# Triangular inverses of an RWKV-7 layer: half of each stream's blocks cross to the other column half

## The reference, cut to what matters

```python
def step(S, inp):
    r_t, w_t, k_t, v_t, a_t, b_t = inp
    sa = jnp.einsum('bhij,bhj->bhi', S, a_t)
    S = S * w_t[:, :, None, :] + sa[..., None] * b_t[:, :, None, :] + v_t[..., None] * k_t[:, :, None, :]
    return S, jnp.einsum('bhij,bhj->bhi', S, r_t)
```

## Time and profile before

| | us |
|---|---|
| median of 3 runs | 769.61 |
| the runs | 768.45, 769.61, 1230.0 |
| profiled execution | 766.94 |
| its span | 764.9 |
| first pair of inverses | from about 122.5 to 150.1 |
| second pair | from about 149.2 to 176.7 |

### The profile page before, as it was taken

One profiled execution on the slowest core, in us unless ns is written; L12 is line 12 of the kernel. 1 busy time (PEld: TensorE's weight loads), 2 busy tenths in 40 slices (PEclk: granted clock), 3 DMA queues, 4 the chain that ended last, 5 costly groups with the idle time before them and its releaser, 6 DMA issues.

```text
span 764.9 us, 18829 instructions
## 1 busy us (share of the span) xinstructions
PE 739.7 (97%) x7940; PEld 694.8 (91%) x7940; DVE 510.9 (67%) x780; ACT 378.5 (49%) x584; POOL 70.4 (9%) x50
## 2 busy tenths in 40 slices
PE   7999999998999999999999999998999999999997
PEld 6988888987879999999999999875689999999997
DVE  4896985677453788785555677776657887854441
ACT  6656454211443545554444435759966554543331
POOL 0000005090130000000000010015410000000000
PEclk9999999999999999999999999999999999999999
DMA  9954330000111589867666563500055666576651
GB/s 298 275 172 135 97 100 27 5 3 2 58 57 56 164 213 254 236 198 219 194 192 194 168 189 111 166 1 2 2 161 169 198 188 198 186 221 194 194 163 56
DMA packets 111038, 109.25 MB, mean 143 GB/s; under 512 B 7264, under 2 KB 109920, under 8 KB 110848
## 3 DMA queue, kind: packets, MB, share of 16 engines
q1 hardware_dynamic: 110976, 108.35, 47.3%
HBM read 107.29 MB, written 1.05 MB: 142 GB/s over the span
## 4 chain that ended last, share of the span: by engine, by line
PE 87%; DVE 6%; ACT 5%; issue 1%; DMA 1%; POOL 1%; ACTq 0%; SPq 0%; POOLq 0%; DVEq 0%
PE ps L460 66%; PE ps L676 4%; ACT SB L1469 2%; DVE Gs L1722 1%; PE ps L773 1%; ACT PT L1480 1%; PE ps L575 1%; PE ps L762 1%; PE ps L988 1%; PE ps L1007 1%; DVE LT L1748 1%; PE ps L558 1%; DMA xtok<-in_x 1%; POOL t L2141 1%; PE ps L491 1%
## 5 line engine op out<-in xcount | busy, mean ns | idle before, releaser
L1537 DVE TENSOR_TENSOR wlo<-raw,whi 128x1024 fp32r<-128x1024 f32 x188 | 225.9, 1224 | 87.9 <-ACT whi L1130 85.6
L1130 ACT ACTIVATE whi<-raw 128x1024 fp32r<-128x1024 f32 x124 | 130.3, 1058 | 127.3 <-PE ps L460 122.4
L460 PE MATMUL ps<-xh,whi 128*128 128x256 f32 x896 | 178.1, 280 | 1.9 <-DVE xl L2100 1.0
L460 PE MATMUL ps<-xl,whi 128*128 128x256 f32 x896 | 175.4, 277 | 0.0
L460 PE MATMUL ps<-xh,wlo 128*128 128x256 f32 x896 | 175.2, 277 | 0.0
L460 PEld LDWEIGHTS ps<-xh,whi 128*128 128x128 f32 x896 | 135.4, 188 | 6.0 <-issue 4.8
L460 PEld LDWEIGHTS ps<-xl,whi 128*128 128x128 f32 x896 | 135.5, 188 | 0.0
L460 PEld LDWEIGHTS ps<-xh,wlo 128*128 128x128 f32 x896 | 135.3, 188 | 0.0
L1365 ACT ACTIVATE whi<-raw 128x1024 fp32r<-128x1024 f32 x64 | 68.0, 1063 | 78.1 <-PE ps L460 57.3
L460 PE MATMUL ps<-hl,whi 128*128 128x256 f32 x512 | 99.8, 276 | 0.0
L460 PE MATMUL ps<-hh,whi 128*128 128x256 f32 x512 | 99.7, 276 | 0.0
(11 more groups left out here) (310 smaller groups left out, 967.3 us busy)
## 6 DMA issues: line engine op xcount, KB each, us to landing
raw<-in_mlp_w SPq DMA_DIRECT2D x128, 512.0 KB, 4.5
raw<-in_rwkv_w_in SPq DMA_DIRECT2D x24, 512.0 KB, 4.8
raw<-in_nsa_w_in SPq DMA_DIRECT2D x20, 512.0 KB, 4.5
raw<-in_rwkv_w_out SPq DMA_DIRECT2D x8, 512.0 KB, 3.5
raw<-in_nsa_w_out SPq DMA_DIRECT2D x8, 512.0 KB, 3.5
cw<-in_nsa_cmp_w SPq DMA_DIRECT2D x4, 512.0 KB, 9.3
cst<-in_consts SPq DMA_DIRECT2D x1, 1047.0 KB, 11.1
xtok<-in_x SPq DMA_DIRECT2D x2, 512.0 KB, 4.2
```

The lines of the kernel that those rows point to most:

```text
L460: last = mm(ps[:, bank0 + m, 0:T], w[:, slot, c0:c0 + P], x_[:, kk, :], start=(kk == 0 and n == 0), stop=(kk == ktiles - 1 and n == 2))
L1130: A(whi[:, s, :], raw[:, s, :], ACT.Copy).then_inc(hi_ready, 1)
L1537: v.tensor_tensor(wlo[:, slot, :], raw[:, slot, :], whi[:, slot, :].bitcast(f32), ALU.subtract)\
```

## The change

- sq2, add2, sq3 and add3 are *crossed*: positions 0 to 3 write where they did, positions 4 to 7 write the other half of the PSUM partitions (head `e` to half `1 - e`) and the next bank. The positions are issued in the order 0, 4, 1, 5, 2, 6, 3, 7, so that four matmuls in a row use four different quadrants. After sq2 and add2 positions 4 to 7 lie on exchanged halves, after sq3 and add3 they are back.
- A crossed result lies in two banks, 256 columns in each; ScalarE copies it with one instruction (`inv_copy2`), and VectorE turns sq3 with one instruction out of both banks. Banks are now fixed by the table `INV_BANK`.
- add2 and add3 no longer add: VectorE writes `LU = LT + I` (`add_unit`, 128x512, both inputs in SBUF) after turning the square, TensorE multiplies the product by that, and ScalarE copies the result. For each stream VectorE so loses two `add_to_product` and gains two `add_unit`, and ScalarE gains two copies.
- VectorE's order in a pair is now: turn and `add_unit` for stream 0, the same for stream 1; turn and `add_unit` for stream 0, the same for stream 1; the turn of sq3 for both; add4 as before.
- GpSimd's and SyncE's lists are as before.

```diff
+    INV_BANK = {"L": 0, "sq1": 1, "sq2": 2, "add2": 0, "sq3": 2, "add3": 0, "add4": 2, "m32a": 3, "m32b": 0, "m64a": 1, "m64b": 2}
-    NINV, NDVE, NACT, NPOOL = 11, 13, 5, 2
+    NINV, NDVE, NACT, NPOOL = 11, 13, 7, 2
+    LU = [place(f"LU{n}", [P, NP_, C], off(12 + n, 6144)) for n in range(2)]
...
-            def times(s, pair, name, lhs, which):
+            def times(s, pair, name, lhs, which, crossed=False):
 
                 bank = inv_bank(s, pair, name)
-                for p in range(NP_):
+                for p in [i + j for i in range(NP_ // 2) for j in (0, NP_ // 2)]:
                     for e in range(2):
-                        last = mm(ps[at(e), bank, p * C:(p + 1) * C], lhs[s][at(e), p, :], DP[s][at(e), p, which, :],
+                        to = 1 - e if crossed and p >= NP_ // 2 else e
+                        b, c0 = (bank + p // 4, p % 4 * C) if crossed else (bank, p * C)
+                        last = mm(ps[at(to), b, c0:c0 + C], lhs[s][at(e), p, :], DP[s][at(e), p, which, :],
                                   start=True, stop=True)
                 last.then_inc(sem(f"inv_pe{s}"), 1)
...
                 for s in both:
                     act_did(s, 2)
                     dve_did(s, 4)
-                    times(s, pair, "sq2", LT, 0)
-                    times(s, pair, "add2", LT, 1)
+                    times(s, pair, "sq2", LT, 0, crossed=True)
+                    dve_did(s, 5)
+                    times(s, pair, "add2", LU, 1, crossed=True)
                 for s in both:
                     act_did(s, 3)
-                    dve_did(s, 5)
-                    times(s, pair, "sq3", LT, 0)
                     dve_did(s, 6)
-                    times(s, pair, "add3", LT, 1)
+                    times(s, pair, "sq3", LT, 0, crossed=True)
+                    dve_did(s, 7)
+                    act_did(s, 4)
+                    times(s, pair, "add3", LU, 1, crossed=True)
                 for s in both:
+                    act_did(s, 5)
                     dve_did(s, 8)
                     times(s, pair, "add4", LT, 1)
...
+            def inv_copy2(s, pair, name, which):
+                act.wait_ge(sem(f"inv_pe{s}"), NINV * pair + INV[name])
+                bank = 4 * s + INV_BANK[name]
+                A(DP[s][:, :, which, :].rearrange("p (b k) n -> p b k n", b=2),
+                  ps[:, bank:bank + 2, 0:GW].rearrange("p b (k n) -> p b k n", n=C), ACT.Copy).then_inc(sem(f"inv_act{s}"), 1)
...
-                for name in ("sq1", "sq2", "m32a", "m64a"):
+                for s in range(2):
+                    inv_copy(s, pair, "sq1", DP[s][:, :, 0, :])
+                for s in range(2):
+                    inv_copy2(s, pair, "sq2", 0)
+                    inv_copy2(s, pair, "add2", 1)
+                for s in range(2):
+                    inv_copy2(s, pair, "add3", 1)
+                for name in ("m32a", "m64a"):
                     for s in range(2):
                         inv_copy(s, pair, name, DP[s][:, :, 0, :])
...
+                def add_unit(s):
+
+                    v.tensor_tensor(LU[s][:, :, :], LT[s][:, :, :], cc("eye64").unsqueeze(1).broadcast_to([P, NP_, C]), ALU.add)\
+                        .then_inc(sem(f"inv_dve{s}"), 1)
...
                 for s in range(2):
                     after_act(s, 2)
                     turn_over(s, DP[s][:, :, 0, :])
+                    after(s, 4)
+                    add_unit(s)
                 for s in range(2):
                     after_act(s, 3)
+                    turn_over(s, DP[s][:, :, 0, :])
                     dve.wait_ge(sem(f"inv_pe{s}"), NINV * pair + INV["add2"])
-                    turn_over(s, DP[s][:, :, 0, :])
-                    add_to_product(s, DP[s][:, :, 1, :], "add2")
+                    after(s, 6)
+                    add_unit(s)
                 for s in range(2):
-                    dve.wait_ge(sem(f"inv_pe{s}"), NINV * pair + INV["add3"])
-                    turn_over(s, inv_out(s, pair, "sq3"))
-                    add_to_product(s, DP[s][:, :, 1, :], "add3")
+                    dve.wait_ge(sem(f"inv_pe{s}"), NINV * pair + INV["sq3"])
+                    after(s, 7)
+                    bank = 4 * s + INV_BANK["sq3"]
+                    v.transpose(LT[s][:, :, :].rearrange("p (b k) n -> p b k n", b=2),
+                                ps[:, bank:bank + 2, 0:GW].rearrange("p b (k n) -> p b k n", n=C)).then_inc(sem(f"inv_dve{s}"), 1)
                 for s in range(2):
+                    after_act(s, 5)
                     add_to_product(s, DP[s][:, :, 1, :], "add4")
```

More of the change, by code:

```diff
@@ L657, in inv_bank @@
             def inv_bank(s, pair, name):
-                return 4 * s + (NINV * pair + INV[name] - 1) % 4
+                return 4 * s + INV_BANK[name]
             def lower_products(s, pair):
@@ L729, in _ @@
                 for s in both:
-                    act_did(s, 4)
+                    act_did(s, 6)
                     dve_did(s, 10)
@@ L737, in _ @@
                 for s in both:
-                    act_did(s, 5)
+                    act_did(s, 7)
                     dve_did(s, 12)
@@ L1292, in inv_copy @@
                 act.wait_ge(sem(f"inv_pe{s}"), NINV * pair + INV[name])
-                bank = 4 * s + (NINV * pair + INV[name] - 1) % 4
+                bank = 4 * s + INV_BANK[name]
                 A(dst, ps[:, bank, :].rearrange("p (k n) -> p k n", n=C), ACT.Copy).then_inc(sem(f"inv_act{s}"), 1)
+            def inv_copy2(s, pair, name, which):
+                act.wait_ge(sem(f"inv_pe{s}"), NINV * pair + INV[name])
+                bank = 4 * s + INV_BANK[name]
+                A(DP[s][:, :, which, :].rearrange("p (b k) n -> p b k n", b=2),
+                  ps[:, bank:bank + 2, 0:GW].rearrange("p b (k n) -> p b k n", n=C), ACT.Copy).then_inc(sem(f"inv_act{s}"), 1)
             for pair in range(NPAIR):
```

## The result

The changed kernel takes **778.87 us** (median of 12 runs, 777.9 to 786.42); the kernel before took 770.43 beside it (12 runs). The ratio is **1.0135, interval 1.0105 to 1.0165**; it is taken from undisturbed runs alone (one of before's took 1230.0), so it isn't the quotient of the medians. Predicted were 769.4, in a range of 765.0 to 773.5: the forecast was wrong, and by its sign too, since the profiled execution should have come out 0.1 shorter.

The account below looks back on a forecast made before the run. TensorE's products were taken to bound each pair's middle, VectorE close behind. Pair 1's -2.1 and pair 2's +0.8 gave -1.3 us (768.3), or about -0.1 with a clock fall (769.5); predicted 769.4, range 765.0 to 773.5.

Parts of the forecast that it names:

- its sign: Whole kernel: the profiled execution was to come out about 0.1 us shorter, with a clock fall counted.
- part 3: VectorE's unit additions wait for GpSimd: one stop of 2.9 us in pair 2, making that pair 0.8 us longer.
- The memset costs nothing, I take it: Pair 2: stream 1's first unit addition, at 159.40 under GpSimd's memset, was taken to run unstretched.
- Rival 2: Pair 2: two unit additions stopped by GpSimd, price 8.5 to 8.9 us, total 774.3; chance 0.12.
- Its other form: Pair 2: stream 0's second unit addition comes 0.78 us later than worked out, after 161.53, and waits to about 165.6.
- the prediction's clock term: Pair 2: TensorE idle during the stop lowers the clock to 1.2 GHz, costing 0 to 1.7 us, 1.2 taken.
- A crossed product: Squares and additions 2 and 3 on TensorE: some 0.65 us long, 0.46 from one start to the next.
- Rival 3: TensorE: crossed products no faster, 0.94 us each; together +0.8 us, total 770.4; chance 0.09.
- The lock rule: VectorE operations with two SBUF inputs wait until about 0.14 us before GpSimd's operation ends; turns and PSUM-input sums don't.
- VectorE's queue in pair 1: Pair 1: with faster products VectorE is the bound, its turns and unit additions running to 136.20, sq3's turns to 137.55.
- The size of a single stop: Pair 2: stream 1's second unit addition starts 2.9 us late, lasting about 3.6 us.
- part 2: VectorE's and ScalarE's new work in the pairs: gain of 2.1 us a pair, as long as VectorE isn't stopped.

Follow-up runs that it names:

- experiment 2: Changed kernel with GpSimd's three wide operations held until after stream 1's second unit addition of pair 2, memset left in place; 769.07 us, ratio 0.999.
- experiment 5: Changed kernel with one GpSimd wait, on the memset's own semaphore, between the memset and the first wide operation; 770.98 us, ratio 1.0028.
- experiment 6: experiment 1 without the crossing, each product on two quadrants again; 769.54 us, ratio 1.0006.
- experiment 1: Changed kernel with GpSimd's memset and wide operations held until after stream 1's second unit addition of pair 2; 769.3 us, ratio 1.0004.
- experiment 4: Changed kernel with 11, 5 and 4 idle TensorE products ahead of the late unit products of pair 2; 778.12 us, ratio 1.012.
- experiment 7: experiment 1 with two idle products fewer ahead of each of pair 1's first squares; 767.93 us, one profiled execution only.

## Why the prediction was wrong

**The step that failed** is in part 3: "The memset costs nothing, I take it". The memset by itself doesn't cost anything (experiments 2, 5). But the sentence priced it by memsets with no reader behind them, and here a reading operation stands directly behind it without a wait: the addition under it lost 5.58 us, and the stops came to 11.7 in place of the 2.9 of the sum. Rival 2 named the place, stream 1's first addition, and had the mechanism wrong ("if the memset does hold") and the price too low: it let the addition go at the memset's end, 161.42, and had two stops of 8.5 to 8.9. In fact the addition went a whole operation later, so that two more found L2196 and L2198: 11.7. Its other form, stream 0's second addition coming too late, did not happen by itself: the 0.08 us of room was 0.13 in experiment 5 (160.59 to 160.72).

**The clock** did fall behind the stops. For one stop I had 1.2 us out of 0 to 1.7; 17 us at the 1.2 GHz level cost 1.95, since until 174.99 the stage waited for the stops anyway. After the one stop of experiment 5 it didn't fall. That doesn't test the prediction's clock term: I had reckoned with some 3 us of TensorE idle in one piece, as before the fall of the earlier trace rows (2.89), and there a break of 1.17 came first and left 1.63 behind the stop. Whether one idle stretch of 3 us there would have lowered the clock stays open.

**Right** were, with their numbers:
- A crossed product: 0.65 long predicted, 0.69 measured. Two that follow each other undelayed are not in the trace after (VectorE paces them). In experiment 2 they are, 0.47 and 0.49 from one start to the next, where 0.46 was predicted. Rival 3 is out: without crossing, products start 0.93 apart (experiment 6).
- The lock rule from the earlier trace rows: the two-input operation starts 0.13 to 0.14 before the end of GpSimd's, and turns stay at 0.70. The Trainium skill's SBUF — State Buffer page ("SBUF: two separate sides") calls it an exclusive lock that a two-input VectorE operation meets at a GpSimd operation that reads SBUF. The traces agree; they add that the reader can hold it before its recorded start, behind a memset.
- VectorE's queue in pair 1. Its unit additions end at 133.28, 134.91, 136.34 and 137.76; predicted, moved by the 1.41 that the stage starts later, were 133.27, 134.89, 136.25 and 137.61. The size of a single stop was right too, where a trace had just one (experiment 5).

**Mis-sized**: part 2's 2.1 us a pair. Without stops the pairs gained 1.05 and 1.30 (experiment 1). From the last unit addition's end to the start of add4's sum pair 1 took 2.72 us instead of 1.86; where no break falls into this stretch (pair 2 of experiments 1, 4 and 5) it takes 2.03. So the break in add4 costs 0.7 of what is missing, and the other 0.3 or so is that I had this stretch 0.17 and VectorE's queue 0.15 too short. In pair 2 of experiment 1 the break ahead of add4's last 12 records costs 0.46:

```profile
165.06 0.56 PE L680 MATMUL ps<-DP,LT 64*64 64x64 f32 x12 [0.62 <-issue]
```

From the last unit addition to the end of the pair it is 12.49 there and 12.03 in experiment 5, which has no such break. I had counted the products' time and not the rate at which their instructions come.

**The total**: in the stage, 11.7 of stops and 1.95 of clock, less a gain of 1.05 in pair 1 and 1.75 in pair 2 (the 1.3 of experiment 1 and the 0.46 of its break, which the changed kernel doesn't have there), come to 10.8. The stops count in full. The medians differ by 8.4, as before's runs spread upwards from 766.57 while most of after's lie near 778; this is read from the lists of times and not tested.

Left open is also when GpSimd's next operation goes ahead of a waiting addition. Between its mask multiplications, which follow each other without a wait, VectorE does get in: in pair 2 after, L1778 was ready at 152.89 and ran from 153.10, 0.14 before the recorded end of the first multiplication, and the second is recorded from 153.20. There the operation in front is itself a reader; behind the memset it wasn't. No run puts the three wide operations in a row without waits. Open too: why matmuls of the MLP are 5 ns longer in some runs at the same granted clock, and whether the unit constant added from PSUM would escape the lock as the old sums did; that wasn't tried.

## What to carry to other kernels

Before moving a sum from "one input in PSUM" to "both inputs in SBUF", lay GpSimd's timeline beside VectorE's: each such operation waits until a reading GpSimd operation ends, several of these in a row turn one stop into a chain of stops, and a memset ahead of the first is no shelter unless GpSimd waits behind it. Here one wait more on GpSimd, placed where the work isn't needed yet, took the stops away (experiment 1). When products become twice as fast, ask what else feeds them: the next limits were VectorE's queue and the arrival of TensorE's instructions.

## What the runs showed of the hardware

- **A GpSimd reader queued behind a memset without a wait keeps a two-input VectorE addition waiting during the memset already.** 6.27 us for an addition of 0.69 (the timeline after); with one wait on the memset's semaphore between them, 0.69 (experiment 5).
- **TensorE's instructions come in blocks.** The page of the profile after counts 48 packets and 0.79 MB on the instruction queue, 16 KB each. Over the traces of the changed kernel and experiments 1 and 7, the breaks in this stage are at instructions 2753, 4033 and 4289 of TensorE's list (weight loads, matmuls and the sequencer's recorded waits counted), whose distances are multiples of 256. A fetch ends 1.3 to 1.5 us before work resumes each time, and it began 3.6 us or more after the one before it, which at the closest is some 14 ns an instruction for blocks of 256. Ordinary products use one per 14.7 ns (0.94 us for 64) and keep pace; crossed ones use one per 7.5 ns ((0.69 - 0.21) / 64), and after eight of them the break cost 0.7. That blocks are the cause of the break is argued from these numbers and from experiment 7, where it moved by eight records with the list.
- **32 matmul records of 64x64 on four quadrants** take 0.69 us, against 1.10 to 1.15 on two (experiment 6).
